# Two transformer-like blocks on one core: the last HGRN head by token halves, S5's turns in one transfer each, and a last output block by token quarters

## The reference

```python
def reference(x, p, ...):
    # first block
    u = rms_norm(h, norm_mix_w);  xa, ga, qb, fb, ib, gb = split(u @ w_in)
    ya = rg_lru(causal_depthwise_conv(xa)) * silu(ga)            # 512 channels
    yb = hgrn2_branch(qb, fb, ib, gb)                            # 4 heads of 128, chunks of 64 tokens
         # o = gla_chunked(...);  o = o * rsqrt(mean(o*o) + eps) * norm_w;  yb = o * silu(g)
    h = h + concat(ya, yb) @ w_out
    h = h + sigmoid(rms_norm(h) @ w_ple_gate + b) * (p @ w_ple_proj)
    x = rms_norm(h, final_norm_w)
    # second block
    h = rms_norm(x) * (1 + sc1) + sh1;  z = h @ w_in_2           # GLA, mLSTM, S5 and gates
    y_s5 = gelu(s5_ssm(su));  y_s5 = y_s5 * sigmoid(y_s5 @ s5_glu_w + s5_glu_b)
    merged = g0 * (y_gla @ proj_gla) + g1 * (y_ml @ proj_ml) + g2 * (y_s5 @ proj_s5)
    x = x + (1 + gt1) * rms_norm(merged @ w_out_2)
    h = rms_norm(x) * (1 + sc2) + sh2
    gate, up = split(h @ ffn_w_in_2)                             # hidden 2816 = 22 x 128
    return x + (1 + gt2) * rms_norm((silu(gate) * up) @ ffn_w_out_2)
```

## Time and profile before

| | us |
|---|---|
| median of 3 runs | 2291.01 |
| lowest and highest | 2290.31, 2293.83 |
| the profiled execution | 2298.25 |
| its span | 2296.5 |
| PE busy | 2238.3 |
| DVE busy | 1052.6 |
| POOL busy | 1152.6 |
| ACT busy | 612.9 |

### The profile page before, as it was taken

How to read it: one execution, slowest core, us unless ns; L and a number is a source line. 1 busy time by engine, 2 the same in 40 slices (tenths; PEclk the granted TensorE clock), 3 DMA queues, 4 the chain that set the end, 5 groups by cost and what they waited for, 6 DMA issues and landing times.

```text
span 2296.5 us, 29717 instructions
## 1 busy us (share of the span) xinstructions
PE 2238.3 (97%) x11256; PEld 1809.2 (79%) x11256; DVE 1052.6 (46%) x1192; ACT 612.9 (27%) x708; POOL 1152.6 (50%) x1106
## 2 busy tenths in 40 slices
PE   7999998999999999999999999999999999999996
PEld 5788887787788787787878788777888888888885
DVE  7888872356633341351586246456432101223306
ACT  6543342335432231121122232243211000111111
POOL 3332224666543222222683343666666676666675
PEclk9999999999999999999999999999999999999998
DMA  6234422232421111111243334424323333323343
GB/s 227 78 110 179 160 92 81 85 99 85 154 74 37 56 56 55 47 56 64 84 120 119 105 124 153 158 92 156 101 92 99 101 101 101 100 95 97 119 156 119
DMA packets 79128, 240.35 MB, mean 105 GB/s; under 512 B 8496, under 2 KB 17856, under 8 KB 79040
## 3 DMA queue, kind: packets, MB, share of 16 engines
q1 hardware_dynamic: 69824, 220.25, 28.8%
q10 hardware_dynamic: 9216, 18.88, 2.3%
HBM read 209.73 MB, written 29.36 MB: 104 GB/s over the span
## 4 chain that ended last, share of the span: by engine, by line
PE 85%; DVE 3%; issue 3%; POOL 2%; ACT 2%; POOLq 1%; DMA 1%; ACTq 1%; DVEq 1%; SPq 0%
PE PG L612 40%; PE PG L653 17%; PE PG L699 15%; PE PG L1061 5%; POOL WL L532 1%; PE PG L1073 1%; PE PX L804 1%; POOLq L531 1%; PE PX L728 1%; PE PX L799 1%; DVE WK L1755 1%; PE PX L810 1%; PE PX L782 0%; DVE PX L1761 0%; SPq L471 0%
## 5 line engine op out<-in xcount | busy, mean ns | idle before, releaser
L532 POOL TENSOR_TENSOR WL<-WRAW,WH 128x1024 fp32r<-128x1024 f32 (+2 forms) x304 | 703.4, 2314 | 45.1 <-issue 0.9
L529 POOL TENSOR_TENSOR TOUCH<-TOUCH 128x2 f32<-128x2 f32 x304 | 83.5, 275 | 1068.6 <-PE PG L699 359.5
L612 PE MATMUL PG<-UL,WH 128*128 128x512 f32 x1072 | 417.9, 390 | 0.0
L612 PE MATMUL PG<-UH,WH 128*128 128x512 f32 x960 | 377.2, 393 | 4.0 <-DVE H L2107 2.4
L612 PE MATMUL PG<-UH,WL 128*128 128x512 f32 x960 | 374.2, 390 | 0.0
L530 POOL TENSOR_SCALAR WH<-WRAW 128x1024 fp32r<-128x1024 f32 (+2 forms) x304 | 310.9, 1023 | 0.0
L612 PEld LDWEIGHTS PG<-UL,WH 128*128 128x128 f32 x1072 | 201.6, 188 | 43.4 <-issue 1.9
L653 PE MATMUL PG<-UH,WH 128*128 128x512 f32 x576 | 226.4, 393 | 3.1 <-DVE WK L1865 1.6
L699 PE MATMUL PG<-UH,WH 128*128 128x512 f32 x544 | 225.3, 414 | 2.2 <-POOL WL L532 2.2
L653 PE MATMUL PG<-UH,WL 128*128 128x512 f32 x576 | 224.1, 389 | 0.0
L653 PE MATMUL PG<-UL,WH 128*128 128x512 f32 x576 | 224.1, 389 | 0.0
(11 more groups left out here) (485 smaller groups left out, 3455.8 us busy)
## 6 DMA issues: line engine op xcount, KB each, us to landing
WRAW<-up_w SPq DMA_DIRECT2D x88, 512.0 KB, 3.5
ADA<-ada_w SPq DMA_DIRECT2D x24, 1024.0 KB, 5.8
WRAW<-down_w SPq DMA_DIRECT2D x48, 512.0 KB, 3.5
WRAW<-out_w SPq DMA_DIRECT2D x30, 512.0 KB, 3.5
WRAW<-zg_w SPq DMA_DIRECT2D x24, 512.0 KB, 3.5
gates<-STG ACTq DMA_DIRECT2D x24, 512.0 KB, 2.6
WK<-gates SPq DMA_DIRECT2D x24, 512.0 KB, 3.4
WRAW<-gla_w SPq DMA_DIRECT2D x18, 512.0 KB, 3.4
```

The costliest lines, as they stand in the source:

```text
L529: pool.tensor_tensor(TOUCH[:, 0:2], TOUCH[:, 2:4], TOUCH[:, 4:6], ALU.add)
L532: pool.tensor_tensor(WL[:, r, 0:n], WRAW[:, r, 0:n], WH[:, r, 0:n].bitcast(F32), ALU.subtract).then_inc(w_split, 1)
L612: mm = pe.matmul(PG[:, bank, :], w[:, r, P * k:P * k + P], v, start=first and k == 0 and n == 0, stop=last and k == kbs - 1 and n == 2)
```

## The change

The parts, in the order of the program:

1. The last HGRN head's norm works on halves of 512 tokens: two squares, two ms matmuls with filler behind each (plan 0.5 and 3.5 instead of 1 and 3), Ln's table loaded ahead of the squares, two Lns, two Exps, two pairs on DVE, two copies and two low parts. The filler's order is changed by `late`: block 7 of tile 0 stands before block 6 of tile 1, and each half of block 7 waits for its own low part.
2. On ACT gate_sigmoid(1, 3) stands ahead of gate_square(1, 2).
3. S5's channels are permuted on the host (by_channel), so that a turn reads 128 partitions with one DMA; turn_in is written in pieces of 512 bytes.
4. The four glu tiles run whole, one after another, behind one wait for all four low parts.
5. half_as_made takes blocks 0 to 5 of both tiles, then 6 and 7 of both.
6. The down tiles have 8, 7 and 7 blocks.
7. The last output block's second half of the tokens is computed in two quarters of 256 tokens (last_part), each in its own PSUM bank; so are the ones matmuls, rs, the products with rs, the residual and the output. The tiles' split order is unchanged: both quarters' blocks 0 to 7 go first, then the first quarter's other 14 blocks, then the second's, these from two tiles that both stay in their slots. POOL takes three output blocks instead of two, in quarters, and DVE five instead of six. 

```diff
@@ tensor, products_by_block (first block, last HGRN head)
+                if late:
+                    parts[-3:-1] = [(kbs - 1, 0), (kbs - 2, 1)]
 ...
                         for half in range(2):
+                            if late and half and k == kbs - 1:
+                                pe.wait_ge(ready, count + k + 2)
@@ tensor, la_core
+                    if by_halves:
+                        for half in range(2):
+                            pe.wait_ge(la["sq"], i * nh + hh + 1 + half)
+                            pe.matmul(PX[:, 2 + half, :], ONES[:], WK[:, sqo, 512 * half:512 * half + 512],
+                                      start=True, stop=True).then_inc(la["ms"], 1)
+                            filler()
+                        continue
@@ tensor, plan of the last head
-                        (1, 0, 2, 1, 0, 1, 3) if last else (2, 0, 2, 2, 0, 1, 1))
+                        (1, 0, 2, 1, 0, 0.5, 3.5) if last else (2, 0, 2, 2, 0, 1, 1), last)
@@ scalar, hg_head
+                if last:
+                    act.activation(vec("scratch", 0), vec("one"), ACT.Ln)
+                    for h in range(2):
+                        act.wait_ge(hg["o"], 4 + h)
+                        act.activation(WK[:, 4, half_tok(h)], PX[:, h, :], ACT.Square).then_inc(hg["sq"], 1)
...
@@ scalar, gate stage
+            gate_sigmoid(1, 3)
             gate_square(1, 2)
-            gate_sigmoid(1, 3)
             gate_square(1, 3)
@@ sync, turn_in; scalar, s5_turned
-                for l in range(8):
-                    sp.dma_start(WK[16 * l:16 * l + 16, 6, :].rearrange("c (g n) -> c g n", n=P), x[l]
-                                 ).then_inc(s5["u_in"], 16)
+                sp.dma_start(WK[:, 6, :], turn_in[T * i:T * i + T, :].rearrange("(q g) n -> q (g n)", g=8)
+                             ).then_inc(s5["u_in"], 16)
...
-                for g in range(8):
-                    act.dma_start(WK[16 * g:16 * g + 16, 12, :].rearrange("c (l n) -> c l n", n=P), y[g]
-                                  ).then_inc(s5["y_in"], 16)
+                act.dma_start(WK[:, 12, :].rearrange("p (l n) -> p l n", l=8),
+                              turn_out[ds(i * T, T), :].rearrange("(l p) n -> p l n", l=8)).then_inc(s5["y_in"], 16)
@@ tensor, glu tiles
-            first_products(TILE0["glu_w"], 4, lambda k: (GH[:, k, :], GLO[:, k, :]), glu_lo, 0, UNIT0["glu_w"] // 2)
-            for n in range(2, 4):
+            pe.wait_ge(glu_lo, 4)
+            for n in range(4):
@@ tensor, out2a and up0
+            def half_as_made(t, hi, ready, count):
+                for k0, k1 in ((0, 6), (6, KB)):
+                    for r in range(2):
+                        pe.wait_ge(w_split, t + r + 1)
+                        for k in range(k0, k1):
+                            pe.wait_ge(ready, count + k + 1)
...
@@ tensor, down_pair
-                                pe.wait_ge(ffn_lo, 22 * hf + min(8 * q + 8, 22))
...
+                                pe.wait_ge(ffn_lo, 22 * hf + (8, 15, 22)[q])
+                                partial(i * 12 + (TILE0[down] + o), o % 2, 2 * n + b, (8, 7, 7)[q],
@@ tensor, the last output block
+                    def last_part(v, q, k0, k1):
+                        pe.wait_ge(w_split, TILE0[down] + 21 + q + 1)
+                        for k in range(k0, k1):
+                            tok, at = slice(256 * v, 256 * v + 256), (0, 8, 15)[q] + k
+                            xh, xl = HH[:, at, tok], hl(at)[:, tok]
+                            for n, (w, x) in enumerate(((WH, xh), (WH, xl), (WL, xh))):
+                                mm = pe.matmul(last_tile(v), w[:, (q + 1) % 2, P * k:P * k + P], x,
+                                               start=at == 0 and n == 0, stop=at == 21 and n == 2)
...
+                        last_part(0, 0, 0, 8)
+                        last_part(1, 0, 0, 8).then_inc(tile_done, 1)
...
+                        last_part(0, 1, 0, 7)
+                        last_part(0, 2, 0, 7).then_inc(tile_done, 1)
+                        last_part(1, 1, 0, 3)
+                        last_square(0)
+                        last_part(1, 1, 3, 7)
+                        last_part(1, 2, 0, 7).then_inc(tile_done, 1)
+                        last_square(1)
@@ scalar, the end
+            for v in range(2):
+                if v:
+                    load_ln()
+                last_squares(v)
+                if not v:
+                    load_ln()
+                last_root(v)
@@ vector, the end
+            for v in range(2):
+                rs = WK[:, 19, quarter(v)]
+                dve.wait_ge(norm_rs, 14 + 2 * v)
+                for j in (4, 5, 6, 7, 3):
...
```

More of the change, by code:

```diff
@@ L301, in out_gate, with quarter, last_tile, last_mean @@
         return TMP[:, 1, :] if i % 2 else WK[:, 5, :]
+    def quarter(v):
+        return slice(512 + 256 * v, 768 + 256 * v)
+    def last_tile(v):
+        return PX[:, 2, 0:256] if v else PG[:, 3, 0:256]
+    def last_mean(v):
+        return PX[:, 3, 0:256] if v else PX[:, 1, 0:256]
     def h_pair(h, u):
@@ L583, in _ @@
             pool.wait_ge(x_reloaded, 16 * KB)
[L584 to L589, removed]
+            for v in range(2):
+                pool.wait_ge(norm_rs, 14 + 2 * v)
+                for j in range(3):
+                    y = YF[1][:, j, 256 * v:256 * v + 256]
+                    pool.tensor_tensor(y, y, WK[:, 19, quarter(v)], ALU.mult)
+                    pool.drain()
+                    pool.tensor_tensor(XR[:, j, quarter(v)], XR[:, j, quarter(v)], y, ALU.add).then_inc(last_out, 1)
         @block.tensor
@@ L1304, in hg_head @@
                     hg_forget(i + 1)
-                la_rest(hg, i, 1, 4, 6)
+                if last:
[3 more added lines that the diff above has]
+                        act.activation(WK[:, 4, half_tok(h)], PX[:, h, :], ACT.Square).then_inc(hg["sq"], 1)
+                    for h in range(2):
+                        act.wait_ge(hg["ms"], 4 + h)
+                        act.activation(WK[:, 6, half_tok(h)], PX[:, 2 + h, :], ACT.Ln, bias=vec("eps"), scale=1.0 / P)
+                    act.drain()
+                    for h in range(2):
+                        act.activation(WK[:, 6, half_tok(h)], WK[:, 6, half_tok(h)], ACT.Exp, scale=-0.5
+                                       ).then_inc(hg["rs"], 1)
+                else:
+                    la_rest(hg, i, 1, 4, 6)
                 if not last:
@@ L1320, in _ @@
             hg_head(3, True)
-            act.wait_ge(hg["y"], 4)
-            act.activation(UH[:, KB - 1, :], H[:, KB - 1, :], ACT.Copy).then_inc(sp_hi, 1)
+            for h in range(2):
+                act.wait_ge(hg["y"], 4 + h)
+                act.activation(UH[:, KB - 1, half_tok(h)], H[:, KB - 1, half_tok(h)], ACT.Copy).then_inc(sp_hi, 1)
             for j in range(2):
@@ L2749, in layout @@
     down = np.zeros((3 * D, D), np.float32)
-    down[:hidden] = f["ffn_w_out_2"][0]
+    for n, (r0, r1) in enumerate(((0, 8 * P), (8 * P, 15 * P), (15 * P, hidden))):
+        down[D * n:D * n + r1 - r0] = f["ffn_w_out_2"][0][r0:r1]
     down = pack_weight(down).reshape(KB, P, 3, D).transpose(0, 2, 1, 3).reshape(3 * KB, P, D)
```

170 lines of the change are left out of this document (95 added, 75 removed).

## The result

| | before | after |
|---|---|---|
| median of 5 runs, us | 2291.01 | 2279.70 |
| lowest to highest | 2288.09 to 2295.86 | 2275.77 to 2281.79 |
| the profiled execution, its span | 2298.25, 2296.5 | 2281.79, 2280.0 |

The ratio is 0.9947 (95% interval 0.9931 to 0.9964): the medians lie 11.3 us apart, where the forecast was 20 us and 2271. The range held the time. Between the two profiled executions the difference is 16.5 us of span, so there are two questions: which terms were mis-sized, and how much of what the runs and the profiles show is the change.

The account below looks back on a forecast made before the run. PE, busy for 2238.3 of 2296.5 us, was taken to bound the kernel. The terms summed to 19.9 us, taken off the median of 2291.0 to give 2271, with a range of 2262 to 2284.

Parts of the forecast that it names:

- 0.15 for a restart: Glu tiles: each of two PE restarts costs 0.15 us, taken off the gain, leaving 2.4 us.
- The pitch of the quarters: Last block: 132 matmuls of 256 columns at 0.120 us each, 0.9 us lost; wrong if above 0.15.
- the rival of 188 ns per load: Last block: weight loads bound the 256-column matmuls, 9.0 us more, 2280; chance 0.12.
- that of the ones matmuls' rate: Last block: quarter matmuls take 0.45 us each, 44 us more, 2315; chance 0.05.
- The row that the forecast leant on: S5's 128-column matmuls, read as 16 with fresh weights in 1.81 us, 0.113 each, so loads can follow that fast.
- the last block on PE: End in quarters: 6.4 us won behind PE, less 1.0 for ones matmul and type changes and 0.9 for pitch; net 4.5.
- out2a: Block order at out2a: 0.4 us won if the clock stays up, 1.0 to 2.4 lost if it falls; taken as -0.6.
- the rival on moved waits: HGRN end, S5, out2a: waits move instead of going and the clock falls behind them, 6.6 us worse, 2278; chance 0.17.
- the -1.4 of a contended split: At out2a: a contended split costs 0.8 us more, which would put out2a at -1.4.
- Two of the three splits shrink to 3.4: Down tiles of 8, 7, 7: two splits shrink to 3.4 us beside a 7-block tile of 4.8; down gain 3.3.
- 2.5 us for stretches at 0.50: Slow clock gone behind removed waits: 1.2 us at the HGRN end and 1.3 after S5's first turn.
- Signs of being wrong: Whole kernel: pitch above 0.15, PE waiting over 5 us in new places, or as many 0.50 windows as before.

Follow-up runs that it names:

- no_hg_halves: The changed kernel with the last HGRN head's norm on whole rows of 1024 tokens again: 40.98 us from 330 to 372 against 37.02.
- sum_late: The changed kernel with the last block's four ones matmuls for earlier squares issued after the first quarter's blocks 8 to 14: ratio 0.9930.
- glu_by_block: The changed kernel with the first two glu tiles by blocks as before, low parts waited for singly: 30.10 us from 1290 to 1320 against 27.43.

## Why the prediction was right, and where it was short

**The mechanisms held.** For four parts undone alone the stage lost what it had gained: HGRN 4.0 to 4.9 (forecast 4.4 with the clock), turns 5.4 to 5.5 (4.9), glu 2.7 (2.4), down tiles 3.5 to 3.6 (3.3). The gate tiles, not tested alone, gave 0.5 (1.0): PE's wait went from 2.41 to 1.49, and 0.44 came back at the next sum of squares (L603 before, L616 after), where the wait for DVE grew from 0.37 to 0.81. The forecast took it that the square moved behind had slack; whether it is the square or POOL's split beside DVE's additions that makes them late wasn't separated. Its 0.15 for a restart was too small as well: the two waits of the glu tiles are 2.11 us and their stage is 2.67 longer, so 0.28 each.

**The pitch of the quarters was 0.120 us, as taken.** In a window of their own the 256-column products run from 2246.80 to 2252.47, 48 starts 0.12 apart:

```profile
2246.80:2252.40 5.60, 5.60 (x47) 1.00 0.77 260
```

So neither the rival of 188 ns per load nor that of the ones matmuls' rate came about. The row that the forecast leant on was misread: L1027's 16 records in 1.81 us are eight matmuls on f32, two records each. But each record has a weight load of its own, and that was all the argument needed. By the Trainium skill ("TensorE: Matmul & The Clock Gate", Back-to-back issue gap) it would be 262 cycles, as an estimate 0.109 us; the row is 10% above it and decides. The prediction put that price at half a microsecond less than its own 0.120; for 132 products it is 1.4.

**The step that failed is that of the last block on PE**, "one more ones matmul ... 1.0" and "0.9 lost", net 4.5. It priced the sums' matmuls and not their place. In before they stood ahead of the last tile, 11 us behind the block's first product; here they stand 5.9 us behind it, and DVE's sum needs 7.8. The wait it adds (1.95) had to be named: it is visible in the code as a wait for norm_acc that moved forward by a tile. How long DVE takes to the sum hangs on how its additions meet POOL's split: in no_hg_halves they took 4.8 us in all instead of 6.4, and PE waited 0.97. With the slow clock after it 3.6 us of the 4.5 were lost. sum_late, with 29.5 us for the block, has 4.4 of the 4.5, but that is in part luck: 5.8 instead of 6.4 behind PE's last product, and on PE 1.4 lost instead of 1.9, since the additional ones matmul cost 0.43 and no row shows the 0.5 for changes of type.

**out2a** was given -0.6 and measured -1.3: the wait for tile 1's WL (1.2) and for tile 2's (2.6, forecast 2.9) came as described, and the clock fell after it, as the rival on moved waits had it. That rival was right here, and wrong at the HGRN end and at up0 (0.1 us). Tile 2's WL took 2.35, as fast as a quiet one, so the -1.4 of a contended split didn't come about either; -1.3 is the loss with the stretch. Where the clock stayed up (glu_by_block) the stage took 0.2 less than before, as the forecast's 0.4 had it; but before paid for a stretch of its own there, and at the same clock the part is a loss of 1.3 to 1.5.

**A wrong reason with the right number.** "Two of the three splits shrink to 3.4": every down tile is loaded and split at 8 blocks, in the changed kernel too, and only PE's part is 7. The 3.5 us come from the shortest tile's 4.8 instead of 4.1 us beside a split that is as long as before.

**Profile and median.** The sum was laid against an execution at a mean clock of 0.990 and then taken off the median of runs at 0.992 to 0.993. It held 2.5 us for stretches at 0.50 that the two removed waits would take along. They did disappear in the profiles, at 367 and 1194. But the stage from 575 to 1150, which no edit touches, took 568.6 to 569.3 us in the four profiles with two stretches, 570.2 and 570.9 with three, 572.4 with four, 574.8 and 575.0 with five, and 575.0 to 576.7 in three with six: some 1.5 us for each, and up to 8 us by chance between two profiles.

Equal mean clocks are no fair measure of the change either. At 0.995 the runs of before take 2286.8 and 2288.2 us, those of the changed kernel 2275.8, 2276.0 and 2276.2: 11 to 12 us. But the mean takes in the end of the program, where PE has nothing left to do and the clock is at 0.50 for 14.0 us in before and for 7.6 after, first before, then after:

```profile
2283.00:2296.00 13.00, 0.00 (x0) 0.00 (x0) 8.23 (x12) 2.82 (x4) 5.02 (x4) 0.50 0.43 161
```
```profile
2273.00:2279.00 6.00, 0.00 (x0) 0.00 (x0) 3.72 (x9) 0.00 (x0) 3.80 (x6) 0.50 0.65 218
```

That end lowers before's mean by 0.0030 and the changed kernel's by 0.0017, so at the same mean before has fewer stretches in which PE works, by nearly two. An estimate from these numbers: at the same number of stretches the change gives some 14 us. The profiles agree: of their 16.5 us two stretches fewer (nine and seven) are 3.0, which leaves 13.5. The two series of runs, 11.3 and 15.5, lie on both sides. That the timed runs of before hold fewer stretches than its profiles is read from their mean clock alone; no trace of them exists.

**Signs of being wrong.** Of the prediction's three the pitch and the number of stretches (seven, where before had nine) stayed clear. PE's waits in new places add up to 6.6 us (1.95 at the sums, 1.21 and 2.57 at out2a, 0.86 behind up0's tiles), more than its 5, though 4.1 of that it had forecast itself. And a wait of 0.41 for WL is left in the down stage, where it allowed 0.3.

## What to carry to other kernels

When a block of work is moved or made in another order, each small operation inside it has its own wait, and each is to be priced again at its new place by the time at which its operand is ready. Two tiles that end together leave the next tile's preparation uncovered: keep a few products of one tile behind the other's end (13.1 us instead of 15.1 here). Before subtracting a sum made in one profile from the median of runs, compare their mean clocks, and leave out the end of the program, where PE is idle.

## What the runs showed of the hardware

- The granted clock falls in stretches of 3.4 us (or 6.8) to 0.50, the lower of two levels (1.2 of 2.4 GHz). Whether one follows a given wait isn't fixed: behind a wait of 2.57 us at out2a it came in seven profiles of eight, behind 2.29 in two of three, behind 1.9 to 2.0 in the last block in three of five, and behind 0.8 and 1.0 there in none of two.
- In the stage from 575 to 1150, with no wait of PE above 1.1 us, two to six times 3.4 us came in each of twelve profiles, but always at the same five places of the program: by the time in before at 614 to 617, 862 to 867, 897, 931 and 1070 us. Which of the places have one changes from profile to profile; what sets the places was not tested.
- Nearly all of the spread between runs of before, 2286.8 to 2299.9 us, goes with the mean clock, 0.995 to 0.989; the six runs at 0.992 still lie 3.4 us apart.
- A DVE addition of two 128x512 operands takes 0.70 us; begun beside POOL's WL of 128x1024 (2249.00 to 2251.66) it took 2.72 and ended 0.54 after it. POOL's WL took 2.35 alone and 3.46 beside DVE's 128x1024 operations.
- 512 KB turned through DRAM in one DMA of 128 partitions hold ACT's queue for 0.41 us, in eight of 16 partitions for 3.7 to 5.0. The single one landed a median of 4.0 us after its issue, the eight 3.0, and DVE, the reader, waited no longer for it (13.4 us in all, 16.2 before).
